# Two halves of weights ahead of the jump into the rest of a large expert body, and the jump back announced ahead of the first down unit

## What is computed

```python
def grouped_moe(h, router_w, router_b, w_gate, w_up, w_down):
    logits = (t @ router_w).astype(jnp.float32) + router_b
    aff = jax.nn.softmax(logits, axis=-1)
    ...
    for e in range(N_EXPERTS):
        hid = jax.nn.silu(t @ w_gate[e]) * (t @ w_up[e])
        y = y + combine[:, e:e + 1] * (hid @ w_down[e])
    return y.reshape(B, S, D)
```

## Time and profile before

| what | value |
|---|---|
| median of three runs | 1766.48 us |
| the profiled execution | 1769.38 us |
| its span | 1767.7 us |
| TensorE's granted clock, mean | 0.933 |
| TensorE busy | 1510.8 us (85%) |
| the experts' stretch | from about 780 us to about 1745 us |

### The profile page before, as it was taken

One profiled execution on the slowest core, in us unless ns is written; L12 is line 12 of the kernel. 1 busy time (PEld: TensorE's weight loads), 2 busy tenths in 40 slices (PEclk: granted clock), 3 DMA queues, 4 the chain that ended last, 5 costly groups with the idle time before them and its releaser, 6 DMA issues.

```text
span 1767.7 us, 27610 instructions
## 1 busy us (share of the span) xinstructions
PE 1510.8 (85%) x12032; PEld 1000.0 (57%) x12032; DVE 584.6 (33%) x1095; ACT 188.8 (11%) x456; POOL 362.5 (21%) x161
## 2 busy tenths in 40 slices
PE   7799999999999999986699955798976666898558
PEld 6588788888888878653444522433433324335223
DVE  0453557877576243431111211113011110212013
ACT  0001012200001100041100100100101001001002
POOL 0005630187677877300000000000000000000000
PEclk9899999999999999988899988898998778899889
DMA  9997896588778654549997899998999999999996
GB/s 386 424 425 218 347 386 263 236 335 353 315 313 351 285 208 179 233 164 427 428 410 280 333 425 427 425 427 356 386 426 426 425 428 426 419 416 414 427 425 266
DMA packets 50926, 629.55 MB, mean 356 GB/s; under 512 B 5763, under 2 KB 8228, under 8 KB 11840
## 3 DMA queue, kind: packets, MB, share of 16 engines
q1 hardware_dynamic: 49192, 621.32, 85.0%
q10 hardware_dynamic: 1560, 5.80, 0.8%
HBM read 623.43 MB, written 3.67 MB: 355 GB/s over the span
## 4 chain that ended last, share of the span: by engine, by line
PE 63%; DMA 31%; issue 2%; DVE 2%; POOL 1%; SPq 1%; ACT 0%; DVEq 0%; ACTq 0%; POOLq 0%
PE bank L1635 23%; PE bank L925 14%; DMA ring<-in_w_up_gate 10%; DMA ring<-in_w_down 9%; PE bank L1397 8%; PE bank L954 6%; DMA region_g<-in_w_up_gate 5%; PE bank L1473 4%; DMA region_g<-in_w_down 4%; DMA ring<-in_ada_w 2%; PE bank L888 2%; PE bank L966 2%; DMA ring<-in_w_in 1%; POOL ring L773 1%; PE bank L961 1%
## 5 line engine op out<-in xcount | busy, mean ns | idle before, releaser
L773 POOL TENSOR_TENSOR ring<-ring 128x1024 f32<-128x1024 f32 x152 | 360.0, 2396 | 329.4 <-DMA ring<-in_w_in 226.7
L925 PE MATMUL bank<-ring,region_b 128*32 128x256 f32 (+1 forms) x3104 | 305.5, 477 | 120.3 <-DMA ring<-in_w_up_gate 94.5
L925 PEld LDWEIGHTS bank<-ring,region_b 128*32 128x32 f32 (+1 forms) x3104 | 129.1, 129 | 278.9 <-issue 142.6
L954 PE MATMUL bank<-ring,region_f 128*32 128x256 f32 (+1 forms) x1920 | 171.0, 449 | 56.3 <-DMA ring<-in_w_down 56.2
L1635 PE MATMUL bank<-ring,region_a 128*128 128x256 f32 x768 | 171.4, 380 | 2.7 <-DVE region_e L2406 2.2
L1635 PE MATMUL bank<-ring,region_x 128*128 128x256 f32 x768 | 170.4, 379 | 0.9 <-issue 0.8
L1635 PEld LDWEIGHTS bank<-ring,region_a 128*128 128x128 f32 x768 | 145.3, 190 | 25.5 <-issue 5.2
L1635 PEld LDWEIGHTS bank<-ring,region_x 128*128 128x128 f32 x768 | 145.3, 190 | 21.1 <-issue 1.1
L954 PEld LDWEIGHTS bank<-ring,region_f 128*32 128x32 f32 (+1 forms) x1920 | 71.2, 122 | 140.8 <-issue 63.8
L2721 DVE TENSOR_TENSOR work<-work,bank 128x128 f32<-128x128 f32 (+1 forms) x32 | 10.3, 321 | 423.1 <-ACT work L1900 423.1
L2208 DVE SCALAR_TENSOR_TENSOR bank<-ring,condT,bank 128x512 f32<-128x512 f32 x192 | 144.8, 754 | 5.8
(11 more groups left out here) (262 smaller groups left out, 1299.9 us busy)
## 6 DMA issues: line engine op xcount, KB each, us to landing
ring<-in_w_up_gate SPq DMA_DIRECT2D x111, 2048.0 KB, 29.5
ring<-in_w_down SPq DMA_DIRECT2D x56, 2048.0 KB, 20.8
ring<-in_ada_w SPq DMA_DIRECT2D x44, 2048.0 KB, 11.8
ring<-in_w_in SPq DMA_DIRECT2D x31, 2048.0 KB, 14.0
region_g<-in_w_up_gate SPq DMA_DIRECT2D x16, 2048.0 KB, 26.1
ring<-in_w_branch SPq DMA_DIRECT2D x8, 2048.0 KB, 14.6
ring<-in_w_out SPq DMA_DIRECT2D x8, 2048.0 KB, 10.5
region_g<-in_w_down SPq DMA_DIRECT2D x8, 2048.0 KB, 30.5
```

Source lines behind the costliest of these rows:

```text
L773: ins = pool.tensor_tensor(quarter(s, *out)[:, k:k + 4, :], quarter(s, *in0)[:, k:k + 4, :], quarter(s, *in1)[:, k:k + 4, :], op)
L925: last = nc.tensor.matmul(bank_of(x, j)[n * c:n * c + n, 0:2 * m], tokens(x, 8 * half + k), w[:, k % 4, :, m * c:m * c + m], start=(half = ...
L954: last = nc.tensor.matmul(bank_of(x, q)[n * c:n * c + n, 0:m], hidT[x][:, k, :], w[:, k % 4, m * c:m * c + m], start=(k == 0), stop=(k == ...
```

## The change

In the two woven bodies the second half of unit 0 for the base (`loaded_half(0, 1)` and `gate_up(0, 0, 0, last)`) goes from the rest into the begin, so it stands ahead of the jump at line 853, the gather and the turn. The first half of unit 1 for the base moves up in the rest, from behind the turns to between the gather and the turn. In `wide` (and in the narrow body, where it changes no order, since begin and rest are one there) the second half of unit 0 goes into the begin too. In all large bodies the announcement of the jump back goes from ahead of unit 5 to ahead of unit 4. Nothing is added or taken away; all other engines' instructions stay in their order.

```diff
@@ woven_begin, woven_units
                 gate_up(0, 0, 0, first)
+                loaded_half(0, 1)
+                gate_up(0, 0, 0, last)
...
                 for x in xs:
                     extra("gather")(x)
-                loaded_half(0, 1)
-                gate_up(0, 0, 0, last)
+                loaded_half(1, 0)
+                gate_up(0, 0, 1, first)
                 for x in xs:
                     extra("turn")(x)
                 turn_weights()
-                loaded_half(1, 0)
-                gate_up(0, 0, 1, first)
                 for x in xs:
                     extra("tokens")(x)
@@ small_begin, units
                 gate_up(base, 0, 0, first).then_inc(half_used, 1)
+                loaded_half(0, 1)
+                gathered((1,))
+                gate_up(base, 0, 0, last).then_inc(half_used, 1)
...
-                    loaded_half(0, 1)
-                    gathered((1,))
-                    gate_up(base, 0, 0, last).then_inc(half_used, 1)
                     gathered((2, 3))
@@ ahead of unit 4, ahead of unit 5
+            announced = pe.mark_branch_hint_location() if base == WIDE else None
             ends = ne == NE - 1 and base == NARROW
...
-            announced = pe.mark_branch_hint_location() if base == WIDE else None
```

## The result

The changed kernel takes 1774.03 us (median of 6 runs, 1771.5 to 1776.6), the kernel before 1766.6 us beside it (6 runs, 1765.78 to 1768.45). The ratio is 1.004 with an interval of 1.0027 to 1.0052: slower by 0.4%, where no change was forecast (1765.1 us, range up to 1769.5).

A forecast was written before the change was run, and what follows sets the result against it. The prediction took the alternating waits of TensorE and DMA as the bound, TensorE's time counting where the DMA starves. Terms 3.85 - 1.25 - 1.05 - 0.2 gave 1.35 us won: 1765.1 us, range 1762.2 to 1769.5.

The forecast's parts named there:

- The new wait: Woven bodies, ahead of the extras' matmuls: TensorE waits for VectorE, 0.9 us in pe0_2, 1.3 in pe1_2 and pe3_0.
- term 3: pe1_2, one_extra: the second half fills the hole, the jump is done as before, extras' matmuls begin 3.85 us earlier.
- the slow clock: pe1_2: gather (3.64 us) and next half (4.73) at 1.2 GHz would run at the high level, 1.85 and 3.58.
- term 2: pe0_2, two_extra: the begin crosses into the next block, its jump's target comes later, and VectorE is awaited: 1.25 us lost.
- term 1: Earlier announcement: no gain; pe1_3's jump back, at slot 12, takes 3.75 us more, 5.5 us of cover, 0.2 lost.
- The fourth rival: pe1_3's late jump back is not covered: up to 4.5 us lost at worst, 1769.4 us; chance 0.08.
- term 4: pe3_0, one_extra: the 0.30 us stall is saved, a 1.3 us wait for VectorE is added: 1.05 us lost.
- term 5: pe1_3, wide: its rest starts in the next block, covered by two halves as before: 0.
- The earlier announcement: Large bodies' jumps back: all four already cost 0.34 us, so announcing them earlier has nothing to win.

The follow-up runs named there:

- slot40: The changed kernel with its large bodies moved 40 slots to the front (`LARGE_SLOT` 40 in place of 80): 1771.64 us, ratio 1.0025.
- early: The changed kernel with the woven bodies' jump to the rest back behind the first half, and unit 1's half cut around the turns: 1768.88 us, ratio 1.0005.
- again: The changed kernel run once more without any edit, for a second trace: 1772.64 us, ratio 1.003.
- no_hint: The changed kernel with fulfilled waits in place of the announcement of the jump to the rest in pe0_2, pe1_2 and pe3_0: 1777.93 us, one run.
- pe13: The changed kernel with 128 never-run instructions each at pe1_3 and pe2_0, moving pe1_3's jump back from slot 12 to 140: 1772.31 us, ratio 1.0029.
- begin_only: The changed kernel with the announcement of the jump back put back to its old place, longer begins kept: 1773.15 us, ratio 1.0032.
- hint_only: The kernel before with only the announcement of the jump back moved ahead of unit 4: 1768.27 us, ratio 1.0001.
- pad: The kernel before with 64 never-run instructions ahead of pe1_3's rest, putting its jump back at slot 12: 1768.52 us, ratio 1.000.
- mixed: split with one half ahead of the jump to the rest in `two_extra` (pe0_2) and two in the other bodies: 1775.29 us, ratio 1.0041.
- mixed56: mixed with `LARGE_SLOT = 56`, all large bodies laid 24 slots earlier, and nothing else: 1768.29 us, ratio 1.0006.
- after: The changed kernel itself, in its first series and profile: 1774.03 us, ratio 1.004.
- split13: The changed kernel with both the cut half of split and the moved jump back of pe13: 1768.46 us, ratio 1.0004.
- ahead: mixed with `one_extra`'s jump to the rest announced in the expert before, next to the announcement of the jump to `more`: 1776.36 us, ratio 1.0046.
- split: The changed kernel with unit 1's half cut in two, 8 matmuls ahead of the turns and 8 behind `turn_weights`: 1768.9 us, ratio 1.0008.

## Why the prediction was wrong

*The new wait* was forecast at 0.9 and 1.3 us and came at 0.85, 1.29 and 1.29. The runs show that it is on the path: filling it gave back 4.4 us, more than its own 3.4 by 1 us, which is within the error of the two ratios. This term was right; the prediction failed in what was to stand against it.

*pe1_2, term 3, is the step that failed: "the jump is done by 1150.8 as before".* 3.85 us were to be won. The forecast let the jump's fetch start where it did before and put a half of work beside it. But the jump itself was the request. Before, it was reached 0.10 us behind the begin's first matmul: TensorE's sequencer handed the 32 instructions of one half on and ran ahead to it. With 64 it is reached at 4.26 us. It isn't the second half's weights that hold it up there: they land 1.4 us earlier (1149.06), and in slot40's pe0_2 3.6 us earlier (885.20, jump at 888.81). Where the weights land late, the jump follows them (slot40's pe1_2: 1153.22, jump at 1153.52). In every trace with two halves in front the array had begun 15 to 20 of their 32 weight loads and 13 to 18 of their 32 matmuls when the jump was reached, so 26 to 36 of the 64 instructions were handed on and not begun. I take it that the queue between sequencer and array holds about one half and not two; no run changes the number of instructions by itself. From there its fetch starts after 3.6 us (1150.45 to 1154.05 in the trace; 4.0 before), the jump is done 10.43 us behind the begin's first matmul and not 6.71, and the gather stood 1.99 us. early, with the jump back in front, shows the other side.

*The same term counted the slow clock as won.* In the profile of before the gather and the half behind it ran at 1.2 GHz, 2.9 us longer than at the high level, and that was to vanish with the hole. In the profile of the changed kernel the first half itself is slow:

```profile
core 0: us, PE busy (x) PEld busy (x) DVE busy (x) ACT busy (x) POOL busy (x), PEclk, DMA share, GB/s
1146.19:1148.19 2.00, 2.00 (x6) 0.83 (x8) 1.00 (x2) 0.00 (x0) 0.00 (x0) 0.50 1.02 434
1148.19:1150.19 2.00, 2.00 (x8) 0.59 (x7) 0.00 (x0) 0.00 (x0) 0.00 (x0) 0.67 1.07 430
```

So the two halves took 8.71 us where 8.1 were forecast. Where the slow stretch falls differs from trace to trace of the same order: on the first half in again, no_hint and pe13 too, on the gather in begin_only, nowhere in slot40. Part of the forecast was also luck of one trace: the old order takes 18.35 and 18.44 us in hint_only and pad, where the profile of before has 19.60. Against these the changed kernel's profile wins 0.0 to 0.1 us in pe1_2 and not 3.85; against the profile of before 1.29. The other traces of its order (again, begin_only, slot40, no_hint, pe13) take 18.52 to 20.63 us and win nothing against hint_only and pad. Even slot40, with no slow clock at all, needs 18.91.

*pe0_2, term 2*: 1.25 us lost were forecast, 1.68 measured (20.58 against 18.90; 1.4 against hint_only and pad), by a reason that was half right. The begin does cross a block, but slot40 reaches the jump as late without crossing. The second half ahead of the jump is enough. That a crossing can delay a jump as much by itself is shown by mixed against mixed56.

*pe1_3's jump back, term 1*: priced at 3.75 us more than now, with 5.5 us of cover, 0.2 lost. It took 7.1 and 5.5 us, and 3.0 and 1.4 us of the DMA's time were lost behind it. The place was right. The price was taken from the nearest row, a jump 29 slots into its block, and is too low; and the cover is too high: of the 6.76 and 5.17 us more than before 3.8 and 3.7 us were covered, and not 5.5. The fourth rival was nearer. In the time of the kernel this is at most some 2 us by pe13.

*pe3_0, term 4*: 1.05 lost forecast, 0.81 measured. *The wide begin, term 5*: 0, as forecast (its jump, to the block that follows, takes 418 ns).

*The earlier announcement* was rightly put at nothing.

In sum: of the forecast's 1.35 us won, 2.6 (against before's own trace) to 3.8 (against hint_only and pad) fall away in pe1_2, 0.4 in pe0_2 and 0 to 2.8 behind pe1_3, and 0.2 come back in pe3_0. That makes 1.5 to 5.5 us lost. Measured are 5.3 and 7.1 us (ratios 1.003 and 1.004). So the terms reach it only at their upper ends. The second table, which counts the DMA's lateness itself, adds up to 4.1 us (after) and 3.0 us (again) against the profile of before, and to 4.4 to 6.7 us against hint_only and pad. What is still missing, up to some 2 us, is no more than traces of one order differ by, and it can't be placed. No version beat the kernel before: split13, early and mixed56 lie within 0.1% of it.

## What to carry to other kernels

A far jump is itself a request for its code, so ask when it is reached, not only what stands ahead of it: here one half in front of a jump let it be reached at once, two halves delayed the request by 4.3 to 5.2 us. When work moves out of a gap to fill another, look what the gap's old occupant covered; here a base half hid 0.85 to 1.29 us of VectorE, and cutting that half in two served both sides. A slow clock seen behind one idle time need not be a cost that goes away with it: compare more than one trace before it is counted as a gain.

## What the runs showed of the hardware

- Of TensorE's instructions, 32 (a base half) let the jump behind them be reached 0.06 to 0.12 us after the first began (mixed's and ahead's pe0_2, at the edge of a block, apart: 4.70 and 5.11); 64 let it be reached at 4.3 to 5.2 us, in every kernel.
- From a jump reached to the start of its code's fetch it takes 3.3 to 4.1 us (before: 4.07, 4.0, 3.7; after: 3.3, 3.6), and from the end of that fetch to the jump's end 1.4 to 1.6 us in every trace. An announcement in the jump's own block was of use only in pe3_0: fetch 1.0 us after the jump (up to 1.9 in other traces), where it was 3.9 without. There it starts 5.8 to 6.2 us behind the fetch of the block that follows, which goes first.
- Two announcements side by side: the earlier had no effect (6130 ns).
- A jump back at slot 12 of its block took 7107, 5517, 5971 and 6075 ns in four traces (after, again, begin_only, no_hint) and 1097 (split) and 433 (pad) in two with the same slot; in the last two its code was fetched 1.4 and 2.9 us ahead of the jump, in the others 3.1 to 4.7 us behind it. What decides which, no run here shows.
